# Weights of two neighbouring 128x128 tiles laid in turn, element by element

## What is computed

```
h  = x + (sigmoid(ga) * (ya @ w_pa) + sigmoid(gc) * (yc @ w_pc)) @ w_o   # ya: chunked attention, yc: short convolution
                                                                     # q, k, v, u, bg, cg, ga, gc = split(n @ w_in + b_in)
h += hier_moe(rms_norm(h))                                           # 32 experts, 2 for each token
h += sigmoid(rms_norm(h) @ w_ple_gate + b) * (p @ w_ple_proj)
hs = concat(meta (16 tokens), h)                                     # 528 tokens
hs += norm(pool_mixer(norm(hs)));  hs += norm(swiglu(norm(hs)))      # layer 0, d_ff = 2816
k, v = kv_in @ w_k, kv_in @ w_v
hs += norm(sliding_window_attention(norm(hs), k, v));  hs += norm(swiglu(norm(hs)))   # layer 1
return hs[16:]
```

## Time and profile before

| | |
|---|---|
| time, median of 3 runs | 1949.32 us (1949.29 to 1949.63) |
| the profiled execution, time | 1950.33 us |
| its span, first to last instruction | 1948.2 us |
| mean granted TensorE clock in it | 0.992 of full speed |
| PE (matmuls) busy | 1888.7 us, 97% |
| PEld (weight loads) busy | 1565.8 us, 80% |
| DVE (VectorE) busy | 917.8 us, 47% |
| ACT (ScalarE) busy | 637.3 us, 33% |

### The profile page before, as it was taken

The page is one execution under the profiler, slowest core; times in us unless marked ns, Lnnn a source line. Parts: engine busy times, 40 slices in busy tenths (PEclk is TensorE's granted clock), DMA queues, the critical chain, the costliest instruction groups (busy, mean ns, idle before and its releaser), DMA issues.

```text
span 1948.2 us, 31374 instructions
## 1 busy us (share of the span) xinstructions
PE 1888.7 (97%) x13564; PEld 1565.8 (80%) x13564; DVE 917.8 (47%) x1611; ACT 637.3 (33%) x1187; POOL 139.8 (7%) x120
## 2 busy tenths in 40 slices
PE   7999999989999999999899999999999999999998
PEld 6866788866666666669789999999867898888898
DVE  5755434233333332247873322447866564423355
ACT  6344323121111011126432222234466543222242
POOL 0022000110000000000000000004222000000001
PEclk9999999999999999999899999999999999999999
DMA  5222242689999999963112232334321213332333
GB/s 190 87 76 76 84 170 96 263 349 429 429 429 430 428 428 428 428 273 99 54 46 87 87 100 83 90 108 142 109 66 55 85 47 108 94 110 82 104 124 115
DMA packets 57149, 345.16 MB, mean 177 GB/s; under 512 B 7168, under 2 KB 7808, under 8 KB 44976
## 3 DMA queue, kind: packets, MB, share of 16 engines
q1 hardware_dynamic: 53184, 334.15, 46.5%
q0 software_dynamic: 3504, 8.54, 1.3%
q10 hardware_dynamic: 320, 0.43, 0.1%
HBM read 343.09 MB, written 4.19 MB: 178 GB/s over the span
## 4 chain that ended last, share of the span: by engine, by line
PE 86%; DVE 7%; DMA 5%; ACT 1%; issue 1%; POOL 0%; DVEq 0%; SPq 0%; ACTq 0%; POOLq 0%
PE bank L487 57%; PE bank L703 9%; PE bank L727 6%; DMA e<-in_we 4%; PE bank L738 1%; PE bank L543 1%; PE bank L739 1%; PE bank L1137 1%; DVE wlo L1321 1%; PE bank L1084 1%; PE bank L920 1%; PE bank L690 1%; PE bank L1056 1%; PE bank L881 1%; PE bank L560 1%
## 5 line engine op out<-in xcount | busy, mean ns | idle before, releaser
L1321 DVE TENSOR_TENSOR wlo<-raw,whi 128x1024 fp32r<-128x1024 f32 x230 | 286.7, 1253 | 127.2 <-ACT whi L2322 123.5
L2322 ACT CAST whi<-raw 128x1024 fp32r<-128x1024 f32 x231 | 239.7, 1043 | 127.3 <-PE bank L487 110.3
L703 PE MATMUL bank<-e,xT 128*64 128x256 f32 x2048 | 234.7, 382 | 1.0 <-DVE xT L1594 1.0
L703 PEld LDWEIGHTS bank<-e,xT 128*64 128x64 f32 x2048 | 143.1, 137 | 80.4 <-issue 11.2
L487 PE MATMUL bank<-nhi,whi 128*128 128x272 f32 (+1 forms) x672 | 191.6, 285 | 1.1 <-DVE sl L1850 0.6
L487 PE MATMUL bank<-nhi,wlo 128*128 128x272 f32 (+1 forms) x672 | 191.2, 284 | 0.0
L487 PE MATMUL bank<-nlo,whi 128*128 128x272 f32 (+1 forms) x672 | 190.6, 284 | 0.0
L487 PE MATMUL bank<-n1hi,whi 128*128 128x512 f32 (+1 forms) x448 | 163.0, 364 | 0.0
L487 PE MATMUL bank<-n1lo,whi 128*128 128x512 f32 (+1 forms) x448 | 160.8, 359 | 0.0
L487 PE MATMUL bank<-n1hi,wlo 128*128 128x512 f32 (+1 forms) x448 | 160.7, 359 | 0.0
L487 PEld LDWEIGHTS bank<-nhi,whi 128*128 128x128 f32 x672 | 127.2, 189 | 2.0 <-DVE sl L1850 0.8
(11 more groups left out here) (397 smaller groups left out, 3768.4 us busy)
## 6 DMA issues: line engine op xcount, KB each, us to landing
e<-in_we SPq DMA_DIRECT2D x94, 2048.0 KB, 22.1
raw<-in_w_down SPq DMA_DIRECT2D x64, 512.0 KB, 3.6
raw<-in_w_gate SPq DMA_DIRECT2D x44, 512.0 KB, 3.5
raw<-in_w_up SPq DMA_DIRECT2D x44, 512.0 KB, 3.6
raw<-in_w_q SPq DMA_DIRECT2D x12, 512.0 KB, 4.4
B<-in_rel POOLq DMA_DIRECT2D x8, 512.0 KB, 4.8
raw<-in_w_gc SPq DMA_DIRECT2D x8, 512.0 KB, 3.6
raw<-in_w_ga SPq DMA_DIRECT2D x8, 512.0 KB, 4.2
```

What stands on the lines that cost most here:

```text
L703: p = e.matmul(b[64 * hf:64 * hf + 64, 0:256], x[:, k, :], W[:, k, 256 * hf:256 * hf + 256], start=(k == 0), stop=(k == 7))
L1321: e.tensor_tensor(wlo[wslot(u)][:], raw[u % NRAW][:], whi[wslot(u)][:].bitcast(F32), ALU.subtract).then_inc(*hit("dve_low", ("lo", u)))
L2322: e.copy(whi[wslot(u)][:], raw[u % NRAW][:]).then_inc(*hit("act_high", ("hi", u)))
```

## The change

The eight tiles of a unit form four pairs. Within a pair the columns of the two tiles now alternate: element 0 of the first, element 0 of the second, element 1 of the first, and so on. `_in_twos` does this on the host, for every weight array whose tiles are stationary operands; `w_v1`, `w_v` and the experts' arrays stay as they are. In the kernel `weight(s)` gives the slice of tile s: it starts at the pair's start plus 0 or 1 and takes every second element, 128 of them within 255. The three places that read tiles use it. Nothing else in the program differs.

```
+    def weight(s):
+
+        o = s // 2 * 256 + s % 2
+        return slice(o, o + 255, 2)
...
-                wh, wl = whi[wslot(u)][:, s * 128:s * 128 + 128], wlo[wslot(u)][:, s * 128:s * 128 + 128]
+                wh, wl = whi[wslot(u)][:, weight(s)], wlo[wslot(u)][:, weight(s)]
                 for o, c0, c1 in outs:
                     for n, (a, x) in enumerate(((wh, hi), (wh, lo), (wl, hi))):
                         i = e.matmul(o, a, x[:, k0 + k, c0:c1], start=(k == 0 and n == 0),
...
+def _in_twos(t):
+
+    *n, p, _ = t.shape
+    return t.reshape(*n, p, 4, 2, 128).swapaxes(-1, -2).reshape(*n, p, 1024)
...
-        "w_q1": _stream(w_in[:, 0:512]), "w_k1": _stream(w_in[:, 512:1024]), "w_v1": _values(w_in[:, 1024:1536]),
+        "w_q1": _in_twos(_stream(w_in[:, 0:512])), "w_k1": _in_twos(_stream(w_in[:, 512:1024])), "w_v1": _values(w_in[:, 1024:1536]),
...
-        "w_kd": _stream(wkd), "w_v": _stream(g["w_v_2"]), "w_q": _stream(g["w_q_2"][0]),
+        "w_kd": _in_twos(_stream(wkd)), "w_v": _stream(g["w_v_2"]), "w_q": _in_twos(_stream(g["w_q_2"][0])),
```

More of the change, by code:

```diff
@@ L3298 @@
         "tokens": np.broadcast_to(np.arange(S, dtype=np.float32), (128, S)), "rel1": rel1, "rel2": rel2,
-        "w_q1": _stream(w_in[:, 0:512]), "w_k1": _stream(w_in[:, 512:1024]), "w_v1": _values(w_in[:, 1024:1536]),
-        "w_u": _stream(w_in[:, 1536:2048]), "w_bg": _stream(w_in[:, 2048:2560]), "w_cg": _stream(w_in[:, 2560:3072]),
-        "w_ga": _stream(w_in[:, 3072:4096]), "w_gc": _stream(w_in[:, 4096:5120]),
-        "w_pa": _stream(g["w_pa"][0]), "w_pc": _stream(g["w_pc"][0]), "w_o": _stream(g["w_o"][0]),
+        "w_q1": _in_twos(_stream(w_in[:, 0:512])), "w_k1": _in_twos(_stream(w_in[:, 512:1024])), "w_v1": _values(w_in[:, 1024:1536]),
+        "w_u": _in_twos(_stream(w_in[:, 1536:2048])), "w_bg": _in_twos(_stream(w_in[:, 2048:2560])), "w_cg": _in_twos(_stream(w_in[:, 2560:3072])),
+        "w_ga": _in_twos(_stream(w_in[:, 3072:4096])), "w_gc": _in_twos(_stream(w_in[:, 4096:5120])),
+        "w_pa": _in_twos(_stream(g["w_pa"][0])), "w_pc": _in_twos(_stream(g["w_pc"][0])), "w_o": _in_twos(_stream(g["w_o"][0])),
         "we": np.stack([g["w1"][0].reshape(NE, 8, 128, 512).transpose(0, 2, 1, 3).reshape(NE, 128, 4096),
@@ L3305 @@
                         g["w2"][0].reshape(NE, 4, 128, 1024).transpose(0, 2, 1, 3).reshape(NE, 128, 4096)], axis=1),
-        "w_ple_gate": _stream(g["w_ple_gate"][0]), "w_ple_proj": _stream(g["w_ple_proj"][0]),
-        "pool_w": np.concatenate([g["pool_w_2"][0][i].reshape(2, 128, 2, 128).transpose(1, 2, 0, 3).reshape(128, 512)
-                                  for i in range(4)], axis=1).reshape(128, 2, 1024).transpose(1, 0, 2),
-        "w_kd": _stream(wkd), "w_v": _stream(g["w_v_2"]), "w_q": _stream(g["w_q_2"][0]),
-        "w_o2a": _stream(g["w_o_2"][0][0:512]), "w_o2b": _stream(g["w_o_2"][0][512:1024]),
-        "w_gate": np.stack([_stream(gu[l][:, 0:DFF]) for l in range(2)]),
-        "w_up": np.stack([_stream(gu[l][:, DFF:]) for l in range(2)]),
-        "w_down0": np.stack([_stream(wd[l][0:1536]) for l in range(2)]),
-        "w_down1": np.stack([_stream(wd[l][1536:]) for l in range(2)]),
+        "w_ple_gate": _in_twos(_stream(g["w_ple_gate"][0])), "w_ple_proj": _in_twos(_stream(g["w_ple_proj"][0])),
+        "pool_w": _in_twos(np.concatenate([g["pool_w_2"][0][i].reshape(2, 128, 2, 128).transpose(1, 2, 0, 3).reshape(128, 512)
+                                  for i in range(4)], axis=1).reshape(128, 2, 1024).transpose(1, 0, 2)),
+        "w_kd": _in_twos(_stream(wkd)), "w_v": _stream(g["w_v_2"]), "w_q": _in_twos(_stream(g["w_q_2"][0])),
+        "w_o2a": _in_twos(_stream(g["w_o_2"][0][0:512])), "w_o2b": _in_twos(_stream(g["w_o_2"][0][512:1024])),
+        "w_gate": np.stack([_in_twos(_stream(gu[l][:, 0:DFF])) for l in range(2)]),
+        "w_up": np.stack([_in_twos(_stream(gu[l][:, DFF:])) for l in range(2)]),
+        "w_down0": np.stack([_in_twos(_stream(wd[l][0:1536])) for l in range(2)]),
+        "w_down1": np.stack([_in_twos(_stream(wd[l][1536:])) for l in range(2)]),
     }
```

## The result

The changed kernel takes 1968.15 us (median, 1965.95 to 1970.66), the kernel before beside it 1949.3 us: a ratio of 1.0102, with a 95% interval of 1.0090 to 1.0114 (the two medians alone give 1.0097). That is **slower by 18.9 us**, where 1894 us and a gain were forecast.

The account below looks back on a forecast made before the run. TensorE's matmul pace was taken as the bound. Gains of 28.2, 24.2 and 11.5 us made 63.9 at best, taken as 55: 1949.3 to 1894 us, with an 8-in-10 range of 1880 to 2043.

Parts of the forecast that it names:

- What bounds the kernel: TensorE's start-to-start pace over 7536 matmuls with own weight loads; one nanosecond on each is 7.5 us.
- the left-over: Start-to-start time beyond one cycle a column: 13.3 ns at 512 and 256 columns, 11.4 in layer 0; forecast 3.1.
- fixed swap cost: Constant price of each weight swap, which the prediction rejected because layer 0's paces vary with start addresses.
- Two reads at one speed: In SBUF, the step-2 load would sweep 9.6 bytes a ns, like the moving operand, so the two stop meeting.
- L500's 3.1 ns: Plain fp32 matmuls at L500 take 216.4 ns for 256 columns, 3.1 over; taken as what the change reaches.
- a count of meetings: In SBUF the faster moving read overtakes the contiguous load and loses some cycles at each meeting.
- 28.2, 24.2 and 11.5 us: Forecast gains on 512 columns, on layer 0's mixture of 272 and 256 and the like, and on aligned 256 columns.
- if the load needs the same time for its 128 elements: Premise that a step-2 weight load still takes 112 ns, sweeping 8 bytes in 0.83 ns.
- No change: Rival: swapping weights needs 13.3 ns however they lie, time 1949.3 us; chance 0.18.
- More collisions: Rival: the load touches twice the places, each costing the moving operand; adds 70 to 94 us; chance 0.22.
- Halved load: Rival: the step-2 load takes 213 ns, so narrower matmuls go to 218 ns, + 466 us, 2415; chance 0.05.
- when only the phase of the meetings moves the wrong way: Rival: a small loss from where the weight and moving reads meet, no time given; chance 0.05.

Follow-up runs that it names:

- e1: Bench, not the kernel: fp32r matmuls with load steps 1 to 8 at four operand offsets; 512 columns, offset 0: 226.9 ns at step 1, 233.1 at step 2.
- e4: Bench, not the kernel: eight operand offsets modulo 256 bytes, broadcast load, plain fp32; 512 columns take 226.7 ns at best with step 1, 230.0 with step 2.
- e5: Kernel before, contiguous loads, with layer 1's activation tiles moved 192 bytes: 1952.48 us, ratio 1.0020.
- e7: Bench, not the kernel: load and moving operand each at steps 0, 1 and 2; 512 columns take 215.9 to 216.6 ns with the moving operand broadcast.
- e9: Bench, not the kernel: 64 to 256 columns behind clock-keeping fillers, load steps 0, 1, 2, 4; load-bound paces 111.7, 111.7, 117.8 and 233.3 ns.
- e3: Kernel before with the alternating layout only for units of 272 and 256 moving columns: 1952.97 us, ratio 1.0021.

## Why the prediction was wrong, step by step

**What bounds the kernel: right.** TensorE's pace sets the time, 7536 matmuls take part, and a nanosecond on each is worth what was said: the paces times the counts gave 19.9 us of the spans' 20.3, which leaves 0.4 us for every other wait.

**That the left-over depends on addresses and isn't a fixed swap cost: right.** e1, e4 and e5 show it, down to the kernel with nothing but a tile moved by 192 bytes. The Trainium skill (TensorE: Matmul & The Clock Gate, "Step-by-step: what each phase is for") says that the two operands have read ports of their own and that a load takes no read bandwidth from a running matmul. The runs don't agree as far as the pace goes: with the same instructions it goes from 226.7 to 233.3 ns at 512 columns by the place of the one operand relative to the other.

**The step that failed** is "Two reads at one speed that have once got out of each other's way don't meet again, and L500 is the row where both run at one speed. The left-over then falls to L500's 3.1 ns". I made a count of meetings out of two speeds, and took L500 as the proof. Both halves fell:

- *Nearly equal speeds had nothing to remove.* With step 2 the two reads run nearly at one speed (8 bytes in 117.8 / 128 = 0.92 ns, against 4 bytes in 0.417 ns: 8.7 and 9.6 bytes a ns), and at none of eight places does the pace at 512 columns fall under 230.0 ns, 16.7 left over (e4). At place 0 the left-over is 20.0 ns with step 2, 13.3 with step 1 and 15.9 to 18.3 with a load that doesn't sweep at all (e4, e7). The difference of the two speeds grows in this order, 0.9, 5.0 and 9.6 bytes a ns, while the left-over first falls and then rises: overtakings don't explain it.
- *L500 doesn't owe its 3.1 ns to equal speeds.* Plain fp32 with a load of step 2, twice as fast in bytes, takes the same 215.8 ns (e4). That the moving operand of L500 is "read at the speed of the load" was an inference from two cycles a column; the rows allow two fast reads as well. What does make this left-over small isn't shown. A small one appears in fp32r only with a moving operand that stands still (2.6 to 3.3 ns, e7), and a slower moving read alone doesn't bring it: with step 2 the moving operand takes two cycles a column and 25.8 ns are left over.

All three terms of the sum, 28.2, 24.2 and 11.5 us, hung on this one step; measured, in their place stand losses of 14.9 us for the first and 5.0 us for the other two together.

**The premise "if the load needs the same time for its 128 elements"** failed by a little: 117.8 against 111.7 ns (e9). This alone would have left 256 columns at 118 and not 112.

**The rivals.** *No change* was wrong about its cause and near in its size at 256 columns. *More collisions* (+ 70 to 94 us) fell: the left-over of 256 columns at aligned places didn't grow at all, and that of 512 grew by 6.7 ns and not by 10 to 13. *Halved load* fell at step 2 and would have been right at step 4. What came is nearest to the case that I had given 0.05 and no time, "when only the phase of the meetings moves the wrong way": the pace depends on how the two reads stand to each other, but meetings weren't found. Before, the 512 columns of layer 1 stood at place 0, the best of the eight places that e4 tried for contiguous loads, and 226.7 ns is a row of that case only. Step 2 has no such place: 230.0 is its best, 233.1 what the kernel's place gives. The other part of the 18.9 us, layer 0's 121.4 to 122.9 ns (+ 4.3 us with the rest of the narrow units, e3), is the same over a mixture of places: e4's rows for the four places give 121.6 and 122.8.

**What the profile of before could have told.** The earlier trace rows show an even 226.7 and 120.0 ns at one place; the scatter of the earlier trace rows shows that other places give other paces. `like_weights` keeps the place at 0 in layer 1. A step that changes the pattern of the load changes where the two reads stand towards each other, and a reader of these rows had to ask first whether the present place is a good or a bad one. I took it for a bad one: I drew from the same rows that there was something to gain.

**Open.** Why the place and the load's step choose 544, 552 or 560 cycles for 512 columns (226.7, 230.0, 233.3 ns at 2.4 GHz), and what the sweeping moving operand meets when the load reads one element, isn't settled: the runs give the sizes and speak against a count of meetings, and no more. So the cause is shown down to a table of paces by step, place and length, and not below it. A moving sweep without any load between the matmuls wasn't tried, nor other data types, nor places finer than 32 bytes.

## What to carry to other kernels

Where each matmul has its own fp32r weight load, measure the pace from start to start and try the difference of the two operands' starts modulo 256 bytes: at 512 columns the places differ by 3% and the aligned one is best, at 256 columns another one is. Keep weight loads contiguous in fp32r: step 2 costs 6 ns on a load of 128 columns and loses the good places that e4 found at 512 and at 256 columns; step 4 doubles the load. And before a small left-over in one row is taken for what a change would reach, change one thing at a time in a bench: the row may owe it to something that the change leaves alone.

## What was not expected of the hardware

- A weight load of step 0, 1, 2 and 4 takes 111.7, 111.7, 117.8 and 233.3 ns for 128 columns in fp32r (e9); with step 8 and 256 moving columns the pace is 242 ns (e1).
- A moving fp32r operand of step 2 takes 452.5 ns for 512 columns, twice 226.7 (e7), while the load of step 2 loses only 6 ns (e9).
- At place 0 a load of step 2 is as good as one of step 1 from 256 to 384 moving columns, costs 1 ns at 448 and 6.2 at 512 (e1).
- Three matmul paces of 512 columns, 216 (moving operand broadcast), 226.7 and 233.3 ns, differ by the addresses read alone, with equal instruction counts and the granted clock at its higher level.
- A tile moved by 192 bytes, with no other edit, made the kernel 0.2% slower (e5).
